# The adaLN product of a hybrid decoder step, spread over four column strips of TensorE

## The chip, the cores and the metric

The kernel runs on one core of a Trainium2 chip. A core has TensorE (matrix products, results in the PSUM memory of eight banks), VectorE, ScalarE and GpSimd (elementwise work; POOL in the profile), and SyncE, whose queue issues the weight loads. The metric is device time in microseconds. TensorE's clock has two levels, 1.2 and 2.4 GHz; the profile shows the granted one as a share of the higher.

## The reference

One inference step of a two-layer trunk for 256 prompt tokens and 8 sequences of 8 sample tokens, all in float32, with D = 1024. Layer 0 is an HGRN2 gated linear recurrence and a dense SwiGLU, layer 1 an S5 state-space mixer and a top-2-of-8 mixture of experts. What matters here is how every sub-layer is modulated:

```python
def _modulation(c, w, b):                       # c: one row per sequence, 1 + 8 = 9 rows
    m = jax.nn.silu(c) @ w + b                  # w: 1024 x 6144, one per layer
    return jnp.split(m[:, None, :], 6, axis=-1) # shift, scale, gate, twice
...
h = _rmsnorm(x, norm_w[layer, 0]) * (1.0 + sc1) + sh1
x = x + g1 * mixer(h)
h = _rmsnorm(x, norm_w[layer, 1]) * (1.0 + sc2) + sh2
x = x + g2 * feed_forward(h)
```

The product silu(c) @ w has 9 rows, a contraction over 1024 and 6144 columns, for each of the two layers.

## The kernel before

Activations are kept transposed: features on the 128 partitions, the 320 tokens along the row. Weights stream from memory through a ring of four slabs, each 128 partitions x 2048 floats (1 MB): eight contraction tiles of 256 output columns. SyncE issues slab n when the first product of slab n - 3 is done (`slab_credit`), so three slabs can be ahead of the one in use.

The adaLN product is cut into 24 pairs of slabs. For each pair q:

- `mod_rows` (line 493) runs twice, once for each half of 256 columns. For each of the eight contraction tiles k it multiplies `siluc[:, k, :]` (128 x 9, the weights of the array) with the slab's tile (128 x 256, streamed) and adds up all eight in PSUM partitions 0 to 8 of one bank. Each float32 matmul is two instructions in the trace, so a slab is 16 and a pair 32.
- ScalarE copies the rows of the bank to `modrow` (line 969, `mod_copy`), which lies in the tile `work`.
- `mod_turn` (line 457, by the helper `tr`) turns four blocks of 9 x 128 into 128 x 9 by a product with the identity, in another bank.
- VectorE adds the bias and writes `mod` (line 1148, `mod_bias`).

The pairs stand in three places of TensorE's order, which is written out by hand:

- Pairs 0 to 3 come at the start, one behind the other. Behind them come the turns of the S5 parameters, the first norm and the HGRN2 input product.
- Pairs 4 to 15 are put between the units of the HGRN2 attention. A unit is one level of a block decomposition of one tile of tokens: VectorE multiplies keys and queries by their decays, TensorE makes the scores (line 607 or 612), VectorE masks them. Units 0 to 3 belong to the sample tokens, 4 to 11 and 12 to 19 to the two prompt tiles. Pairs 4 to 6 follow the scores of units 0 to 2, pairs 7 to 13 those of units 4 to 10, pairs 14 and 15 those of units 12 and 13; a pair's turn stands in the next unit with room. In units 4 to 11 TensorE also makes one head's sample state (line 627, into banks 6 and 7), behind pair and turn, and VectorE adds it before it goes on to the next unit's keys. POOL makes the arguments of the decays up to four units ahead and the mask for line 627; ScalarE takes the exponentials (line 1012).
- Pairs 16 to 23 are put into the S5 loop, one half to each of its 16 steps. There `states_out` (line 750) writes 32 output rows at a time to partitions 32 j to 32 j + 31: four matmuls a step, two for each of two such strips.

Of the kernel before, what the change touches and what calls it, by code (L numbers as in the profile page):

```python
# [20 lines left out]
ACT = mybir.ActivationFunctionType  # L21
AX = mybir.AxisListType

P = 128
D = 1024
KT = D // P
# [6 lines left out]
NC = 1 + NB  # L33
# [10 lines left out]
RING = 4  # L44
# [11 lines left out]
C_KEEP = 392  # L56
C_PAR = 712
C_IOTA = 714
C_W = 842


class Steps:
# [11 lines left out]
def trunk(nc, I, outs, prep):  # L74
    with ExitStack() as ctx:
        def sb(name, shape, dt=F32):
            return ctx.enter_context(nc.sbuf_tensor(name, shape, dt))
# [3 lines left out]
        def sem(name):  # L81
            if name not in sems:
                sems[name] = ctx.enter_context(nc.semaphore(name))
            return sems[name]

        PS = ctx.enter_context(nc.psum_tensor("PS", [P, 8, 512], F32))


        const = sb("const", [P, C_W])
        xT = sb("xT", [P, KT, T])  # L90
        hT = sb("hT", [P, KT, T])
        mod = sb("mod", [P, 96, NC])
        siluc = sb("siluc", [P, KT, NC])
        vecs = sb("vecs", [P, 49])
        adab = sb("adab", [P, 96])
        scale_a = sb("scale_a", [P, KT, NC])
# [4 lines left out]
        work = sb("work", [P, 1024])  # L101
        acts = work[:, 0:2 * T].rearrange("p (s t) -> p s t", s=2)
        gated = work[:, 2 * T:3 * T]
        modrow = work[0:NC, :].rearrange("p (s n) -> p s n", s=2)
        sT = sb("sT", [P, 19, GP])
        ring = sb("ring", [P, RING, SLAB])
        zero16 = sb("zero16", [P, 512], BF16)
# [346 lines left out]
        def _(pe):  # L454
            def tr(out, in_, k):

                return pe.matmul(out, in_, ident[0:k, 0:k], start=True, stop=True)  # L457
# [11 lines left out]
            for k in range(KT):  # L469
                last = tr(PS[:, 5, 16 * k:16 * k + NC], crow[:, k * P:(k + 1) * P], NC)  # L470
            last.then_inc(sem("siluc_psum"), 1)
            pe.wait_ge(sem("ld_x"), 32)
            for i in range(TT):
                for half in range(2):
                    if i == 2:
                        pe.wait_ge(sem("x_turned"), half + 1)
                    for k in range(4):
                        kk = half * 4 + k
                        last = tr(PS[:, 2 * (i % 2) + half, k * P:k * P + TOK[i]],
                                  xin[0:TOK[i], i, kk * P:(kk + 1) * P], TOK[i])  # L480
# [4 lines left out]
            def mod_rows(q, half, bank):  # L485

                n = q * 2 + half
                n += s_mod0 if q in pairs0 else s_mod1 - 8 if q in pairs1 else s_mod2 - 32
                if half == 0 and q:
                    pe.wait_ge(sem("mod_rows_read"), q)  # L490
                arrived(n)
                for k in range(KT):
                    last = pe.matmul(PS[0:NC, bank, half * 256:half * 256 + 256], siluc[:, k, :],  # L493
                                     ring[:, n % RING, k * 256:k * 256 + 256], start=(k == 0), stop=(k == KT - 1))
                    if k == 0:
                        last.then_inc(slab_credit, 1)
                if half:
                    last.then_inc(sem("mod_rows_psum"), 1)

            def mod_turn(q, bank):  # L500
                pe.wait_ge(sem("mod_rows_read"), q + 1)
                if q:
                    pe.wait_ge(sem("mod_ready"), q)
                for c in range(4):
                    last = tr(PS[:, bank, c * NC:(c + 1) * NC], modrow[:, q % 2, c * P:(c + 1) * P], NC)
                last.then_inc(sem("mod_turn_psum"), 1)

            for q in pairs0:
# [8 lines left out]
            for m in range(19):  # L517
                last = tr(PS[:, 4 + m // 10, (m % 10) * GP:(m % 10) * GP + GP], ssr[:, 16 + m, :], GP)
# [16 lines left out]
            for a in range(2):  # L535
                for m in range(2):
                    last = tr(PS[:, 6, (a * 2 + m) * P:(a * 2 + m + 1) * P], x0n[a][:, m, :], P)
            last.then_inc(sem("x0_psum"), 1)

            with pe.Fori(0, 3) as s:  # L540
                for h in range(H):
# [3 lines left out]
                    for k in range(KT):  # L545
                        last = pe.matmul(PS[:, h % 4, 0:T],  # L546
                                         ring[:, h // 2, k * 256 + (h % 2) * P:k * 256 + (h % 2) * P + P],
                                         hT[:, k, :], start=(k == 0), stop=(k == KT - 1))
# [6 lines left out]
            for src in (bexp[0], bexp[1], cexp[0], cexp[1]):  # L555
                for half in range(2):
                    if g >= 4:
                        pe.wait_ge(sem("mats_turned"), g - 3)
                    for k in range(4):
                        last = tr(PS[:, 4 + g % 4, k * P:(k + 1) * P], src[:, half * 4 + k, :], P)  # L560
# [4 lines left out]
            for j in range(4):  # L565
                arrived(s_hin + 12 + j)
                for i in range(TT):
                    pe.wait_ge(sem("hin_credit"), g + 1)
                    for k in range(KT):
                        last = pe.matmul(PS[0:TOK[i], g % 4, 0:256], hT[:, k, i * P:i * P + TOK[i]],  # L570
                                         ring[:, j, k * 256:k * 256 + 256], start=(k == 0), stop=(k == KT - 1))
# [7 lines left out]
            for i in range(TT):  # L579
                for half in range(2):  # L580
                    if g >= 2:
                        pe.wait_ge(sem("kt_ready"), g - 1)
                    for k in range(4):
                        h = half * 4 + k
                        last = tr(PS[0:TOK[i], 6 + g % 2, k * P:(k + 1) * P], hT[:, h, i * P:i * P + TOK[i]], P)
# [3 lines left out]
            for u, (i, L) in enumerate(units):  # L589
                n = TOK[i]  # L590
# [11 lines left out]
                for h in range(H):  # L602
                    kq = ekq[b % 4][:, h, 0:n] if L else None
                    if u in masked:
                        keys, queries = (kq, kq) if L else (x[:, h, i * P:i * P + n] for x in (hk, hq))
                        at = h * n
                        last = pe.matmul(PS[0:n, 2 + at // 512, at % 512:at % 512 + n], keys, queries, start=True,
                                         stop=True, skip_group_check=True)
                        continue
                    for s0 in range(0, P, 2 * L):  # L610
                        c = (h % 4) * P + s0 + L
                        last = pe.matmul(PS[s0:s0 + L, h // 4, c:c + L], kq[:, s0:s0 + L], kq[:, s0 + L:s0 + 2 * L],
                                         start=False, stop=(L == 16 and h % 4 == 3), skip_group_check=True)
# [7 lines left out]
                if u in sample_at:  # L621
# [4 lines left out]
                    for half in range(2):  # L626
                        last = pe.matmul(PS[:, 6 + half, :], hkt[0:64, 2, h * P:(h + 1) * P],  # L627
                                         vmask[0:64, half * 4:half * 4 + 4, :], start=True, stop=True)
# [12 lines left out]
                for part in range(H * n // 512):  # L641
# [3 lines left out]
                    for h in range(part * 512 // n, (part + 1) * 512 // n):  # L645
                        at = (h * n) % 512
                        o = PS[:, 4, at:at + n]
                        last = pe.matmul(o, hv[0:n, i, h * P:(h + 1) * P], scores[0:n, h, 0:n], start=True,
                                         stop=(i == 0), skip_group_check=True)
                        if i == 1:  # L650
                            last = pe.matmul(o, st1[:, h, :], hf[:, h, P:2 * P], start=False, stop=True,
                                             skip_group_check=True)
                        if i == 2:
                            for b in range(NB):
                                last = pe.matmul(o[:, b * NS:(b + 1) * NS], st0[:, b, h, :],
                                                 hf[:, h, NP + b * NS:NP + (b + 1) * NS],
                                                 start=False, stop=(b == NB - 1), skip_group_check=True)
# [11 lines left out]
            for c in range(5):  # L669
                last = pe.matmul(PS[:, c, :], const[:, C_ONE:C_ONE + P], hbflat[:, c * 512:(c + 1) * 512],  # L670
                                 start=True, stop=True)
# [122 lines left out]
            for i in range(TT):  # L794
                n = TOK[i]
# [144 lines left out]
        def _(act):  # L940
# [24 lines left out]
            def mod_copy(q, bank):  # L965
                act.wait_ge(sem("mod_rows_psum"), q + 1)
                if q > 1:
                    act.wait_ge(sem("mod_turn_psum"), q - 1)
                A(modrow[:, q % 2, :], PS[0:NC, bank, :], ACT.Copy).then_inc(sem("mod_rows_read"), 1)  # L969

            for q in pairs0:
                mod_copy(q, q % 2)
# [170 lines left out]
        def _(dve):  # L1143
# [42 lines left out]

            V.memset(epst[:], EPS).then_inc(sem("eps_ready"), 1)
            V.memset(zero16[:], 0.0).then_inc(sem("zeros"), 1)

            dve.wait_ge(sem("ld_ssm"), 48)  # L1190
            dve.wait_ge(sem("dt_ready"), 1)
# [10 lines left out]
            def reduced(out, quarter):  # L1202
# [33 lines left out]
            step(V.tensor_copy(vecs[:], PS[:, 4, 0:49]))  # L1236
            step(V.tensor_copy(adab[:], PS[:, 4, 64:160]))
            dve.wait_ge(sem("siluc_psum"), 1)
            V.tensor_copy(siluc[:], PS[:, 5, 0:128].rearrange("p (k c) -> p k c", k=KT)[:, :, 0:NC])\
                .then_inc(sem("siluc_ready"), 1)  # L1240
            g = 0
            for i in range(TT):
# [435 lines left out]
def constants(np):  # L1678

    c = np.zeros((P, C_W), np.float32)  # L1680
    s = np.arange(P)[:, None]
    t = np.arange(P)[None, :]
    c[:, C_ID:C_ID + P] = s == t
    c[:, C_BEFORE:C_BEFORE + P] = s < t
    c[:, C_ONE:C_ONE + P] = 1
    c[:, C_SAMPLE:C_SAMPLE + NB] = s // NS == t[:, 0:NB]
    keep = np.ones(T, np.float32)
    keep[[0, P]] = 0
    keep[NP::NS] = 0
    c[:, C_KEEP:C_KEEP + T] = keep  # L1690
    c[:, C_PAR:C_PAR + 2] = (s // 16) % 2 == t[:, 0:2]
    c[:, C_IOTA:C_IOTA + P] = t
    return c


# [33 lines left out]
```

## Time and profile before

| | us |
|---|---|
| median of 3 runs | 2364.74 (2363.24 to 2364.99) |
| span of the profiled execution (first to last instruction) | 2361.8 |
| TensorE matmul busy | 1991.8 (84%) |
| VectorE busy | 1209.0 (51%) |
| ScalarE busy | 775.6 (33%) |
| GpSimd busy | 608.9 (26%) |

The time of the profiled execution that is shown is its span; the median of the runs is 2.9 us longer, for what lies around the span. Matmuls are pipelined and their ends modelled, so the durations of single matmuls add up to more than the busy time. Busy shares are means over stages with different limits; what a change in one stage is worth is read from that stage.

### The profile page before, as it was taken

The page shows a single profiled execution, that of the slowest core. Times are in us where ns is not written, and L with a number is a line of the kernel's source. Part 1 is how long each engine was busy: PE and PEld are TensorE (multiplying, and loading weights), DVE is VectorE, ACT ScalarE, POOL GpSimd, SP SyncE. Part 2 cuts the span into 40 slices and gives each one's busy share as a digit, 9 for nine tenths or more (in the row PEclk, how much of TensorE's full clock was granted, in tenths as well). Part 3 has the DMA queues.
Part 4 walks back from the last instruction along what each step waited for, and adds up shares of the span by engine and source line. Part 5 has one row for each costly group of instructions (what it writes and reads, how often), then busy time and mean ns, then how long its engine had stood idle before and what let it go on. Part 6 is the DMA issues. An engine that isn't in the chain of part 4 may idle for free.

```text
span 2361.8 us, 27880 instructions
## 1 busy us (share of the span) xinstructions
PE 1991.8 (84%) x10680; PEld 1510.2 (64%) x10682; DVE 1209.0 (51%) x1486; ACT 775.6 (33%) x813; POOL 608.9 (26%) x308
## 2 busy tenths in 40 slices
PE   5899597665779999566658789999999999999995
PEld 3577463444557767222225579898989898979894
DVE  3300402345220000699991247676767676767675
ACT  1111201011011100111111147575757575757571
POOL 0000201220198000254540003242323232424240
PEclk7799777777789999766668879999999999999998
DMA  5544333320533334121212549898988888888984
GB/s 157 134 116 142 107 107 107 107 76 32 175 104 113 121 105 123 61 72 54 71 54 81 165 133 321 267 320 272 314 285 302 296 298 298 300 297 299 298 301 139
DMA packets 365801, 420.52 MB, mean 178 GB/s; under 512 B 17948, under 2 KB 339757, under 8 KB 365494
## 3 DMA queue, kind: packets, MB, share of 16 engines
q1 hardware_dynamic: 363542, 413.02, 53.5%
q10 hardware_dynamic: 2064, 4.19, 0.6%
q0 software_dynamic: 144, 2.62, 0.3%
q8 instruction: 33, 0.54, 0.1%
q14 instruction: 18, 0.15, 0.0%
HBM read 410.86 MB, written 8.95 MB: 178 GB/s over the span
## 4 chain that ended last, share of the span: by engine, by line
PE 73%; DVE 21%; ACT 3%; issue 2%; DMA 0%; SPq 0%; DVEq 0%; ACTq 0%
PE PS L845 29%; DVE arena L1148 11%; PE PS L697 8%; PE PS L493 5%; PE PS L546 4%; PE PS L457 4%; PE PS L722 4%; PE PS L831 3%; PE PS L784 3%; DVE exact L1148 2%; PE PS L570 2%; DVE arena L1429 2%; DVE hT L1148 2%; PE PS L682 2%; PE PS L527 1%
## 5 line engine op out<-in xcount | busy, mean ns | idle before, releaser
L845 PE MATMUL PS<-exact 128*112 128x256 f32 (+1 forms) x5280 | 774.4, 306 | 19.9 <-DVE exact L1148 19.9
L845 PEld LDWEIGHTS PS<-exact 128*112 128x112 f32 x5280 | 686.9, 175 | 87.8 <-DVE exact L1148 27.7
L1148 DVE TENSOR_TENSOR exact<-arena,exact 128x2048 fp32r<-128x2048 f32 (+1 forms) x162 | 310.9, 1923 | 140.8 <-ACT exact L1087 140.1
L1604 POOL TENSOR_TENSOR arena<-arena 128x512 f32<-128x512 f32 (+4 forms) x154 | 226.4, 1491 | 434.3 <-ACT arena L1056 333.9
L1087 ACT ACTIVATE exact<-arena 128x2048 fp32r<-128x2048 f32 x162 | 309.9, 1913 | 41.5 <-PE PS L845 41.4
L1148 DVE TENSOR_TENSOR arena<-arena 128x128 f32<-128x128 f32 (+7 forms) x399 | 262.1, 709 | 65.4 <-ACT arena L1012 52.2
L1604 POOL TENSOR_TENSOR exact<-arena,exact 128x1024 fp32r<-128x1024 f32 x56 | 192.6, 3446 | 268.3 <-ACT exact L1087 268.3
L1148 DVE TENSOR_TENSOR exact<-ring,exact 128x2048 fp32r<-128x2048 f32 (+1 forms) x104 | 224.9, 2169 | 56.5 <-ACT exact L1087 56.5
L1604 POOL TENSOR_TENSOR exact<-ring,exact 128x1024 fp32r<-128x1024 f32 x32 | 103.9, 3248 | 508.8 <-ACT exact L1087 508.8
L493 PE MATMUL PS<-ring,siluc 128*9 128x256 f32 x768 | 210.7, 441 | 12.5 <-ACT work L969 12.0
L697 PE MATMUL PS<-hT,ring 128*128 128x320 f32 x704 | 191.8, 436 | 14.8 <-DVE hT L1172 14.8
L1087 ACT ACTIVATE exact<-ring 128x2048 fp32r<-128x2048 f32 x104 | 198.0, 1912 | 17.8 <-PE PS L845 17.8
L697 PEld LDWEIGHTS PS<-hT,ring 128*128 128x128 f32 x704 | 134.9, 192 | 71.7 <-DVE hT L1172 15.3
L493 PEld LDWEIGHTS PS<-ring,siluc 128*9 128x9 f32 x768 | 76.2, 102 | 146.4 <-issue 62.8
L1148 DVE TENSOR_TENSOR arena<-arena,PS 112x256 f32<-112x256 f32 (+2 forms) x162 | 79.2, 493 | 97.5 <-PE PS L627 83.5
L457 PE MATMUL PS<-const,arena 112*128 112x112 f32 (+6 forms) x596 | 96.5, 299 | 35.7 <-DVE xT L1245 19.7
L750 PE MATMUL PS<-arena 128*32 128x320 f32 x128 | 36.6, 722 | 98.2 <-DVEq L1434 98.2
L457 PEld LDWEIGHTS PS<-const,arena 112*128 112x128 f32 (+6 forms) x596 | 88.2, 215 | 41.7 <-DVE xT L1245 19.9
L546 PE MATMUL PS<-hT,ring 128*128 128x320 f32 x384 | 105.2, 437 | 0.0
L1148 DVE TENSOR_TENSOR arena<-work,PS 128x320 f32 x22 | 10.7, 488 | 181.8 <-PE PS L697 181.8
L722 PE MATMUL PS<-arena,ring 128*128 128x320 f32 x352 | 95.0, 433 | 1.1 <-DVEq L1403 1.1
L546 PEld LDWEIGHTS PS<-hT,ring 128*128 128x128 f32 x384 | 74.0, 193 | 30.9 <-issue 1.2
(195 smaller groups left out, 1735.1 us busy)
## 6 DMA issues: line engine op xcount, KB each, us to landing
arena<-in_moe_w_in SPq DMA_DIRECT2D x109, 1024.0 KB, 7.5
ring<-in_moe_w_in SPq DMA_DIRECT2D x75, 1024.0 KB, 9.2
arena<-in_moe_w_out SPq DMA_DIRECT2D x56, 1024.0 KB, 5.1
ring<-in_ada_w SPq DMA_DIRECT2D x48, 1024.0 KB, 5.2
ring<-in_moe_w_out SPq DMA_DIRECT2D x33, 1024.0 KB, 7.5
ring<-in_ffn_w_in SPq DMA_DIRECT2D x22, 1024.0 KB, 6.2
ring<-in_hgrn_w_in SPq DMA_DIRECT2D x16, 1024.0 KB, 5.7
ring<-in_ffn_w_out SPq DMA_DIRECT2D x16, 704.0 KB, 5.5
```

The lines of the kernel that those rows point to most:

```text
L457: return pe.matmul(out, in_, ident[0:k, 0:k], start=True, stop=True)
L493: last = pe.matmul(PS[0:NC, bank, half * 256:half * 256 + 256], siluc[:, k, :], ring[:, n % RING, k * 256:k * 256 + 256], start=(k == 0), ...
L546: last = pe.matmul(PS[:, h % 4, 0:T], ring[:, h // 2, k * 256 + (h % 2) * P:k * 256 + (h % 2) * P + P], hT[:, k, :], start=(k == 0), stop= ...
L570: last = pe.matmul(PS[0:TOK[i], g % 4, 0:256], hT[:, k, i * P:i * P + TOK[i]], ring[:, j, k * 256:k * 256 + 256], start=(k == 0), stop=(k ...
L697: last = pe.matmul(PS[:, 2 * (t % 2) + m, 0:T], ring[:, (n + m) % RING, k * 256 + sub * P:k * 256 + sub * P + P], hT[:, k, :], start=(k == ...
L722: last = pe.matmul(PS[:, c, 0:T], ring[:, (n + k // 11) % RING, (k % 11) * P:(k % 11 + 1) * P], mid[:, k, :], start=(k == 0), stop=(k == F ...
L784: last = pe.matmul(PS[:, 2 * sub + m, 0:T], ring[:, (n + m) % RING, k * 256 + sub * P:k * 256 + sub * P + P], hT[:, k, :], start=(k == 0), ...
L831: last = pe.matmul(PS[:, 6 + half, k * P:k * P + CAP], htok[0:TOK[i], i, kk * P:(kk + 1) * P], pick[0:TOK[i], i, :], start=(i == 0), stop= ...
L845: last = pe.matmul(out, a[x], w[y], start=first and m == 0, stop=end and m == 2)
L1087: A(wparts[0][:, j % HRING, :], eslab(j), ACT.Copy).then_inc(sem("rounded"), 1)
L1148: return V.tensor_tensor(out, a, b, op)
L1604: return G.tensor_tensor(out, a, b, op)
```

## The change

The eight contraction tiles of a slab go to four strips of 32 array columns in turn: tile k writes PSUM partitions 32 (k mod 4) to 32 (k mod 4) + 31, and each strip adds up two tiles. For that `siluc` is widened from 9 to 32 columns, the rest zero, cleared once by VectorE. ScalarE copies all 128 partitions of the bank. The turn no longer multiplies with the identity but with a selector: a 128 x 9 block of the constants with a one where partition mod 32 equals the column, so that it turns the rows and adds up the four strips in the same product.

```diff
+C_SEL = 842
-C_W = 842
+C_W = 851
...
-        siluc = sb("siluc", [P, KT, NC])
+        siluc = sb("siluc", [P, KT, 32])
...
-        modrow = work[0:NC, :].rearrange("p (s n) -> p s n", s=2)
+        modrow = work[:].rearrange("p (s n) -> p s n", s=2)
...
                 for k in range(KT):
-                    last = pe.matmul(PS[0:NC, bank, half * 256:half * 256 + 256], siluc[:, k, :],
-                                     ring[:, n % RING, k * 256:k * 256 + 256], start=(k == 0), stop=(k == KT - 1))
+                    strip = 32 * (k % 4)
+                    last = pe.matmul(PS[strip:strip + 32, bank, half * 256:half * 256 + 256], siluc[:, k, :],
+                                     ring[:, n % RING, k * 256:k * 256 + 256], start=(k < 4), stop=(k >= 4))
...
                 for c in range(4):
-                    last = tr(PS[:, bank, c * NC:(c + 1) * NC], modrow[:, q % 2, c * P:(c + 1) * P], NC)
+                    last = pe.matmul(PS[:, bank, c * NC:(c + 1) * NC], modrow[:, q % 2, c * P:(c + 1) * P],
+                                     const[:, C_SEL:C_SEL + NC], start=True, stop=True)
...
-                A(modrow[:, q % 2, :], PS[0:NC, bank, :], ACT.Copy).then_inc(sem("mod_rows_read"), 1)
+                A(modrow[:, q % 2, :], PS[:, bank, :], ACT.Copy).then_inc(sem("mod_rows_read"), 1)
...
             V.memset(zero16[:], 0.0).then_inc(sem("zeros"), 1)
+            step(V.memset(siluc[:], 0.0))
...
-            V.tensor_copy(siluc[:], PS[:, 5, 0:128].rearrange("p (k c) -> p k c", k=KT)[:, :, 0:NC])\
+            V.tensor_copy(siluc[:, :, 0:NC], PS[:, 5, 0:128].rearrange("p (k c) -> p k c", k=KT)[:, :, 0:NC])\
...
+    c[:, C_SEL:C_SEL + NC] = s % 32 == t[:, 0:NC]
```

## Rows read from the trace of the kernel before

**Rows 1.** The page: shares of the chain that ended last, by line.
```profile
PE PS L845 29%; DVE arena L1148 11%; PE PS L697 8%; PE PS L493 5%; PE PS L546 4%; PE PS L457 4%; PE PS L722 4%; PE PS L831 3%; PE PS L784 3%; DVE exact L1148 2%; PE PS L570 2%; DVE arena L1429 2%; DVE hT L1148 2%; PE PS L682 2%; PE PS L527 1%
```
**Rows 2.** The chain in order of time: start, length, engine, tile, line, instructions.
```profile
39.58 9.35 PE PS L493 x32
...
65.64 7.00 PE PS L493 x32
75.32 8.31 PE PS L457 x38
...
313.63 8.69 PE PS L493 x32
```
**Rows 3.** Groups by form, 294 to 540 us: count, busy, mean ns, idle before.
```profile
L493 PE MATMUL PS<-ring,siluc 128*9 128x256 f32 x384 | 93.9, 407 | 0.0
...
L1148 DVE TENSOR_TENSOR arena<-arena,PS 128x1024 f32<-128x1024 f32 x9 | 11.0, 1221 | 83.5 <-PE PS L627 83.5
```
**Rows 4.** The chain through one unit, 381 to 400 us.
```profile
382.56 8.43 PE PS L493 x32
391.00 0.98 PE PS L457 x8
391.98 1.92 PE PS L627 x4
...
394.00 4.97 DVE arena L1148 x3
```
**Rows 5.** Windows: length, busy of five engines, granted clock, DMA share, GB/s.
```profile
1000.00:1258.00 258.00, 155.97 (x535) 61.73 (x533) 238.99 (x428) 38.25 (x129) 123.37 (x84) 0.66 0.18 57
...
1130.00:1135.00 5.00, 2.20 (x8) 0.57 (x8) 4.50 (x14) 0.54 (x4) 1.14 (x1) 0.50 0.00 0
```
**Rows 6.** Timeline of TensorE and its weight loads in one S5 step.
```profile
1132.80 2.35 PE L750 MATMUL PS<-arena 128*32 128x320 f32 x8 [5.60 <-DVEq L1434]
...
1133.34 0.19 PEld L750 LDWEIGHTS PS<-arena 128*32 128x32 f32 x2 [0.34 <-issue]
```
**Rows 7.** Timeline: the scores of unit 6, blocks of 16.
```profile
399.02 0.73 PE L612 MATMUL PS<-arena 128*16 128x16 f32 x64 [5.12 <-DVE arena L1148]
```
**Rows 8.** Timeline: VectorE's first wait, a turn-like product, a ScalarE copy.
```profile
11.11 0.28 DVE L1195 TENSOR_TENSOR arena<-arena 32x128 f32<-32x128 f32 x1 [9.93 <-ACT arena L960]
...
331.31 3.58 PE L655 MATMUL PS<-arena 128*128 128x8 f32 x16
...
359.69 0.60 ACT L1029 ACTIVATE hT<-PS 128x512 f32<-128x512 f32 x1 [36.74 <-PE PS L655]
```
**Rows 9.** The page, DMA issues: KB each, median us to landing.
```profile
ring<-in_ada_w SPq DMA_DIRECT2D x48, 1024.0 KB, 5.2
```
**Rows 10.** Window with a full DMA queue; columns as in rows 5.
```profile
10.00:20.00 10.00, 5.72 (x35) 5.50 (x34) 8.55 (x18) 0.20 (x1) 0.00 (x0) 1.00 0.94 296
```
**Rows 11.** Timeline of SyncE's queue: slab issues, first to last merged.
```profile
40.63 17.95 SPq L321 DMA_DIRECT2D ring<-in_ada_w  x5
...
296.18 23.68 SPq L321 DMA_DIRECT2D ring<-in_ada_w  x6
```
**Rows 12.** Groups by form, 364.4 to 409 us and 419.8 to 486 us.
```profile
L493 PE MATMUL PS<-ring,siluc 128*9 128x256 f32 x96 | 26.2, 441 | 0.0
...
L493 PE MATMUL PS<-ring,siluc 128*9 128x256 f32 x128 | 28.7, 383 | 0.0
```
**Rows 13.** Windows of pairs 7, 9 and 10; columns as in rows 5.
```profile
364.50:373.50 9.00, 9.00 (x34) 3.34 (x33) 0.00 (x0) 0.00 (x0) 0.00 (x0) 0.78 0.55 169
...
399.70:408.10 8.40, 8.40 (x39) 3.07 (x32) 0.50 (x1) 0.00 (x0) 0.00 (x0) 0.83 0.58 184
419.90:427.00 7.10, 7.10 (x34) 2.92 (x34) 0.00 (x0) 0.02 (x1) 0.00 (x0) 1.00 0.69 218
```
**Rows 14.** Timeline: the exponential for unit 7, the scores of unit 7.
```profile
398.44 1.06 ACT L1012 ACTIVATE arena<-arena 128x1024 f32<-128x1024 f32 x1 [6.82 <-POOL arena L1604]
...
416.29 3.65 PE L607 MATMUL PS<-arena 128*128 128x128 f32 x16 [5.25 <-DVE arena L1148]
```

## The prediction

> **What bounds the kernel now.** I read the chain that ended last first. The matmul of line 493, the adaLN product, holds 5% of it [rows 1], so the question is in which of its three places it lies there: before the first norm (pairs 0 to 3), between the units of the attention stage (pairs 4 to 15), or in the S5 loop (pairs 16 to 23). A pair is two weight slabs of 1 MB, 16 matmul instructions each.
>
> Pairs 0 to 3 lie on the chain one behind the other, the first from 39.6 us, the last to 72.6, and the next step after turn and bias starts at 75.3 (first and last of four in [rows 2]). Pairs 4 to 15 take 93.9 us between 294 and 540, and VectorE's state update waits 83.5 us there for the state matmul (line 627), which TensorE issues behind the pair [rows 3]. One unit shows the ring: pair 8.43, turn 0.98, state matmul 1.92, VectorE 4.97, then the next unit's scores [rows 4]. A microsecond off the pair is one off the ring. In the S5 loop VectorE is busy for 239 of 258 us [rows 5]: the pairs there lie beside it, and a shorter pair gives nothing.
>
> **The change, part by part.** *The product.* A pair today is 32 instructions in 7.00 us at the high clock [rows 2]: 0.22 us each, and 0.43 at the low one (1.2 GHz, half of 2.4). They all write one strip of the array's output columns and stand in line. After the change neighbours go to four different strips. Does the chip overlap strips? The S5 output (line 750) writes two strips, 128x320, eight instructions a time. In line they would take 8 x 0.22 x 320/256 = 2.2 us at the high clock, 4.4 at the low. The window shows clock 0.50, and the eight took 2.35 [rows 5, 6]: two at a time, although the code gives all four of one strip first, and the weights of the next two are loaded at 1133.34, when the first two were not yet done. For four strips there are only the 16-column scores: 64 instructions in 0.73 us [rows 7], 11 ns each, where in line at the low clock 16 columns need 27 (430 x 16/256). That is 2.3 at a time at least, and such short ones may be held by issue. Bounds, with 0.2 us for the last to drain: two at a time (3.6 us a pair at the high clock, 7.0 at the low) and four (1.9 and 3.6). I take four, as nothing in the rows limits the streams at two.
>
> The Trainium skill speaks against it ("TensorE: Matmul & The Clock Gate", Part 3, on what overlaps): weight loads overlap running matmuls only when the row group differs, and column strips share all their rows. By that rule the load stands bare. Line 750 shares its rows too, and its loads did not stand bare [rows 6]. The same part measures 2.38 times for three column tiles; as an estimate by that page four would give 3.2, the pair 2.2 us instead of 1.9, and the sum would be 12 x 0.3 = 4 us smaller.
>
> *The rest.* The row copy on ScalarE reads 128 partitions instead of 9; another 128x512 copy takes 0.60 us [rows 8], as this one does. The turn contracts over 128 rows instead of 9: sixteen instructions with 128x128 weights and 8 columns take 3.58 us at the low clock [rows 8], 1.8 for eight, about twice today's 0.98 at the high one [rows 4], so the turn costs what the clock makes it cost and no more. The clearing of siluc (128x256) falls where VectorE waits 9.93 us for its first input [rows 8]; bare, it would be about a third of a microsecond. The constants grow by 9 of 842 columns in a load that is over long before line 493 starts. All at nothing.
>
> *When the pair gets shorter, slabs and clock come next.* A slab lands 5.2 us after its issue [rows 9], and a full queue moves 296 GB/s [rows 10], 3.5 us a slab: 7 us a pair, today's pace of the product. Three slabs wait in the ring when a stretch begins.
>
> **A, pairs 0 to 3.** Slab 3 is issued when slab 0's first product is done, at 40.6 as today [rows 11], and lands at 45.9; with 3.5 each, slab 7 lands at 59.9. Its products (1.9, at the low clock, since TensorE now waits between slabs) end at 61.8. Today's tail, 72.6 to 75.3, is 2.7 us; with 0.8 for slower turns the next step starts at 65.3. Gain 10, bounds 7 (slabs at 4 us) and 13.
>
> **B, pairs 4 to 6.** Slab 3 is issued at 296.2 [rows 11] and lands at 301.4, slab 5 at 308.4; its products end at 309.4 instead of 322.3 [rows 2]. Less a slower turn: gain 12, bounds 9 and 14.
>
> **C, pairs 7 to 13.** Today 26.2 us for the first three and 28.7 for the other four [rows 12]. The granted clock tells why they differ: 0.78 in the first window, 0.83 in the third (the second lies between), 1.00 in the fourth [rows 13]. A window of 9.0 us at 0.78 holds 4.0 us of the low level, one of 8.4 at 0.83 holds 2.9; with the scores ahead (2.0 and 0.7) the clock rose 3.6 to 5.9 us after the unit's first matmul. In the later four the scores alone take 3.65 [rows 14], and the pair finds the high clock. Now the short pair is over before the clock rises in the first three: 26.2 - 3 x 3.6 = 15.4, and I give back half of what a low clock costs the turn (0.8) and the state matmul (1.9), 4 in all. In the later four the rise comes between the pair's start (1.9) and 2.2 us into it (3.0): 28.7 - 4 x 2.5 = 18.7. Gain 30. Bounds: high clock behind every pair, 36.5; low throughout, 54.9 - 7 x 3.6 - 7 x 2.7 = 11.
>
> What is late next in the ring: POOL's arguments and ScalarE's exponential run a unit ahead. The exponential at 398.4 [rows 14] feeds VectorE's products only behind the next state matmul, a unit (17.5 us) after 394.0; with units 5 us shorter some 7 us are left.
>
> **D, pairs 14 and 15.** The last slab is issued about 1.1 us after pair 14 begins at 518.1, lands at 524.4, and its products end at 526 instead of 535.6. Gain 9.5, bounds 6 and 10.5.
>
> Sum: 10 + 12 + 30 + 9.5 = 61.5 us. Span 2361.8 - 61.5 = 2300.3; the median of the runs is 2.9 above the profiled span: **2303 us**.
>
> **Rivals.**
> - *Two strips at a time.* A 8, B 10, C (26.2 - 15.7) + (28.7 - 4 x 4.0) = 23, D 6.5: 47.5 us, 2317. For: the only strips that the trace shows at length are two. Against: [rows 7].
> - *The clock stays low through the attention stage.* A 9, B 9, C 11, D 6, less four later scores at 1.6 more each: 28.5 us, 2336. For: TensorE will be idle for a larger share of each unit, and in today's gaps the clock fell to the low level. Against: scores, pair and state matmul are still some 8 us of matmuls at the low clock, and today's rise came after 3.6 to 5.9.
> - *Strips do not overlap here:* the queue keeps its order and the time is 2365.
> - *Slower: the 32-column weight loads come bare.* Two loads of line 750 take 0.19 us [rows 6]. Loads in line with products in line: 32 x (0.22 + 0.18) = 12.8 us a pair, 5.8 more, on 16 pairs: 2458. It decides from (7.0 - 1.9)/32 = 0.16 us bare per instruction if the streams still overlap; below that the change gains. Against: [rows 6]. The skill's rule above would lead here.
>
> **How the numbers follow.** Four strips with the clock as argued 0.64, two strips 0.10, low clock 0.13, no overlap 0.06, bare loads 0.04, something else slower 0.03. The range reaches from all upper bounds (74 us, 2291) to just short of the low clock's 2336: 2290 to 2332. A measurement of this kernel tells 0.2% (5 us) from no change; all cases with overlap are faster by more: faster 0.87, same 0.06, slower 0.07.
>
> **What would show it.** Matmuls of line 493 starting some 50 ns apart and a pair in 1.9 to 3.6 us. SyncE's slab issues in pairs 0 to 6 some 3.5 us apart, line 493 waiting for slabs there (A, B). Units 4 to 10 each 4 to 5 us shorter, the state matmul still ahead of VectorE's update (C). The S5 loop unchanged at 258 us. I am wrong if line 493 keeps 0.2 us between starts, if state matmul or scores grow by what the pair loses (clock), or if the exponential takes the state matmul's place as VectorE's last wait.

## The result, and the profile after

The change makes the kernel faster: 2294.9 us (median of 4 runs, 2294.33 to 2296.87) against 2364.8, a ratio of 0.9712 [0.9699, 0.9726]. The span fell by 69.0 us, from 2361.8 to 2292.8. The forecast was 2303 (2290 to 2332), so the side, the mechanism and the range held, and 8 us more came than the sum had.

Where the 69 us come from is read by laying the two chains beside each other at places that both have: the start of the same step, in us from the span's start.

| step | before | after | gained up to here | by this stretch |
|---|---|---|---|---|
| turns of the S5 parameters (behind pair 3) | 75.3 | 66.1 | 9.3 | 9.3 |
| HGRN2 input product | 102.4 | 92.8 | 9.7 | 0.4 |
| scores of unit 0 | 294.4 | 283.8 | 10.6 | 0.9 |
| scores of unit 4 (behind pairs 4 to 6) | 362.6 | 340.4 | 22.2 | 11.6 |
| state matmul of unit 11 (behind pairs 7 to 13) | 494.6 | 439.8 | 54.8 | 32.7 |
| outputs of the second prompt tile (behind pairs 14, 15) | 560.9 | 495.1 | 65.8 | 10.9 |
| output product | 601.2 | 535.4 | 65.8 | 0.0 |
| second norm | 642.4 | 575.0 | 67.4 | 1.6 |
| first step of the S5 loop | 998.1 | 928.6 | 69.5 | 2.1 |
| end of the S5 loop | 1257.9 | 1188.5 | 69.4 | -0.1 |

First the product itself. Four lines of the timeline of TensorE and its weight loads answer to [rows 2]: pair 0, then slabs 2, 3 and 7.

```profile
39.47 0.20 PEld L495 LDWEIGHTS PS<-ring,siluc 128*32 128x32 f32 x8 [0.70 <-DVE xT L1249]
39.47 3.64 PE L495 MATMUL PS<-ring,siluc 128*32 128x256 f32 x32 [0.52 <-DVE xT L1249]
39.89 0.20 PEld L495 LDWEIGHTS PS<-ring,siluc 128*32 128x32 f32 x4 [0.23 <-issue]
43.82 1.07 PE L495 MATMUL PS<-ring,siluc 128*32 128x256 f32 x16 [0.72 <-ACT work L972]
47.17 1.94 PE L495 MATMUL PS<-ring,siluc 128*32 128x256 f32 x16 [2.28 <-DMA ring<-in_ada_w]
...
59.80 1.94 PE L495 MATMUL PS<-ring,siluc 128*32 128x256 f32 x16 [1.10 <-DMA ring<-in_ada_w]
61.67 1.88 PE L507 MATMUL PS<-const,work 128*128 128x9 f32 x8
```

At the low clock one instruction takes 0.43 us. Eight weight loads come in the first 0.20 us, and then four more each 0.43 us: four instructions run beside each other, one to a strip, and the next four loads lie under them. A pair takes 3.64 us, a slab 1.94. The product then waits for its slabs, as forecast: the products of slab 3 start at 47.2, where the forecast had it land at 45.9, but slab 7 is done at 61.7 (61.8 in the prediction).

Next the chain in order of time through the attention stage; it answers to [rows 2] and [rows 4].

```profile
285.59 5.42 DMA ring<-in_ada_w
...
291.06 1.07 PE PS L495 x16
...
342.41 2.59 PE PS L495 x32
...
354.05 3.41 PE PS L495 x30
...
366.27 3.51 PE PS L495 x32
369.78 1.81 PE PS L507 x8
371.59 3.72 PE PS L630 x4
375.40 5.10 DVE arena L1151 x3
380.54 3.78 PE PS L610 x16
384.32 2.12 PE PS L495 x32
...
399.44 3.08 PE PS L495 x32
...
415.52 1.88 PE PS L495 x32
...
428.57 2.18 PE PS L495 x32
...
463.17 5.33 DMA ring<-in_ada_w
...
468.55 1.11 PE PS L495 x16
...
535.42 36.21 PE PS L685 x128
...
575.00 6.28 PE PS L530 x16
...
588.50 5.48 DVE hT L1175 x8
```

The ring of a unit is the old one with a shorter pair: pair, turn, state matmul (now line 630), VectorE, next scores. Pairs 7 to 13 took 54.9 us before [rows 12]; now their chain pieces add up to 18.8 (2.59, 3.46 with its first two instructions, which are a piece of their own, 3.51, 2.12, 3.08, 1.88, 2.18). The shortest, 1.88, is a pair wholly at the high clock: 7.00 / 1.88 = 3.7 times faster than in line. Where the clock is low behind the pair, the turn (1.81) and the state matmul (3.72) take nearly twice as long, as in unit 6 here; in unit 7 they take 0.99 and 1.93, as in [rows 4].

The groups by form of 338 to 435 us say what VectorE waits for there: still the state matmul, 50.8 us.

```profile
L1151 DVE TENSOR_TENSOR arena<-arena,PS 128x1024 f32<-128x1024 f32 x7 | 8.6, 1222 | 50.8 <-PE PS L630 50.8
```

Last, windows of the S5 loop and of the first two 3 us of the output product (columns as in [rows 5]).

```profile
535.42:538.42 3.00, 3.00 (x6) 2.02 (x7) 0.00 (x0) 0.00 (x0) 0.00 (x0) 0.50 0.16 31
538.42:541.42 3.00, 3.00 (x13) 2.13 (x12) 0.00 (x0) 0.00 (x0) 0.00 (x0) 1.00 0.96 318
...
930.50:1188.50 258.00, 113.07 (x534) 49.97 (x533) 239.16 (x428) 38.47 (x129) 120.59 (x84) 0.51 0.18 57
```

In the loop TensorE has 43 us less to do (113 against 156), its mean clock fell from 0.66 to 0.51, VectorE is as busy as ever, and the loop takes 259.9 us where it took 259.8 (last two lines of the table).

The 3.7 us behind the attention stage, which no term of the sum had, are in these pieces of the chain of the kernel before, in windows of its output product, and in one window of the second norm's matmuls in each kernel, before and after:

```profile
601.17 37.80 PE PS L682 x128
...
642.35 7.55 PE PS L527 x16
...
657.51 7.11 DVE hT L1172 x8
```
```profile
601.17:604.17 3.00, 3.00 (x6) 2.02 (x7) 0.00 (x0) 0.00 (x0) 0.00 (x0) 0.50 0.14 37
604.17:607.17 3.00, 3.00 (x7) 1.86 (x6) 0.00 (x0) 0.00 (x0) 0.00 (x0) 0.50 0.93 312
...
642.35:646.00 3.65, 3.65 (x7) 2.47 (x8) 0.00 (x0) 0.00 (x0) 3.65 (x3) 0.50 0.82 264
```
```profile
575.00:578.00 3.00, 3.00 (x8) 1.98 (x9) 0.00 (x0) 0.00 (x0) 3.00 (x1) 0.66 0.73 218
```

The output product lost 1.6 us (37.80 to 36.21): the clock rose after 3 us instead of 6. The norm's matmuls lost 1.3 (7.55 to 6.28), and there too the clock rose sooner: the mean granted clock of their first 3 to 4 us was 0.66 instead of 0.50, that of the rest 0.79 instead of 0.70. VectorE's scaling behind them lost 1.6 (7.11 to 5.48). The change touches none of the three. With smaller pieces beside them they come to 4.9 us, of which 1.1 is lost again up to the S5 loop.

For the scaling, the timelines of GpSimd show what ran beside it, before and after:

```profile
661.15 4.44 POOL L1604 TENSOR_TENSOR arena<-arena,sT 128x512 f32<-128x512 f32 x4
```
```profile
589.50 2.73 POOL L1608 TENSOR_TENSOR arena<-arena,sT 128x256 f32<-128x256 f32 x4
```

GpSimd starts work of its own with the second norm in both kernels (at 642.24 and 574.91), in which its instructions grow from 32 to 512 columns. VectorE's eight scalings come behind the norm's matmuls. Before, they started 15.2 us after the norm did, and the last three ran beside instructions of 512 columns, at 1.21 us each. Now they start 13.5 us after it and are done as those begin: 0.88 us at most. In the first norm, where GpSimd is idle, all eight take 2.6 us. So the scaling follows the norm's matmuls, and these follow the clock. It is read from the traces; no run moved GpSimd's work.

### The profile page after: what moved, and what is told of

It is laid out like the page before. It is cut to its first block, busy times and chain, and to the rows that moved or that the text cites. A ratio compares the mean times of both kernels' runs of the same rounds, so it can differ in the third digit from the quotient of the medians.

```text
span 2292.8 us, 27883 instructions
## 1 busy us (share of the span) xinstructions
PE 1871.5 (82%) x10682; PEld 1473.3 (64%) x10682; DVE 1207.8 (53%) x1487; ACT 775.8 (34%) x813; POOL 605.7 (26%) x308
## 4 chain that ended last, share of the span: by engine, by line
PE 71%; DVE 22%; ACT 3%; issue 2%; DMA 1%; SPq 0%; DVEq 0%; ACTq 0%
PE PS L848 30%; DVE arena L1151 12%; PE PS L700 8%; PE PS L549 5%; PE PS L725 4%; PE PS L458 4%; PE PS L834 3%; PE PS L787 3%; DVE exact L1151 2%; PE PS L573 2%; DVE arena L1433 2%; DVE hT L1151 2%; PE PS L685 2%; PE PS L530 1%; PE PS L927 1%
## 5 line engine op out<-in xcount | busy, mean ns | idle before, releaser
L1608 POOL TENSOR_TENSOR arena<-arena 128x512 f32<-128x512 f32 (+4 forms) x154 | 221.4, 1458 | 423.9 <-ACT arena L1059 335.1
L458 PE MATMUL PS<-const,arena 112*128 112x112 f32 (+6 forms) x596 | 97.8, 302 | 34.8 <-DVE xT L1249 18.3
L753 PEld LDWEIGHTS PS<-arena 128*32 128x32 f32 x128 | 9.2, 158 | 170.5 <-DVEq L1438 159.5
L1151 DVE TENSOR_TENSOR arena<-arena,PS 112x256 f32<-112x256 f32 (+2 forms) x162 | 79.1, 492 | 64.9 <-PE PS L630 50.8
L495 PE MATMUL PS<-ring,siluc 128*32 128x256 f32 x768 | 75.7, 544 | 20.6 <-ACT work L972 12.4
```

The source lines that it names most:

```text
L495: last = pe.matmul(PS[strip:strip + 32, bank, half * 256:half * 256 + 256], siluc[:, k, :], ring[:, n % RING, k * 256:k * 256 + 256], star ...
L753: last = pe.matmul(PS[q:q + 32, 4 + k % 2, 0:T], cct[a][:, k, q:q + 32], vb[w % 2][a][:, j, :], start=(a == 0), stop=(a == 1), skip_group_ ...
L1151: return V.tensor_tensor(out, a, b, op)
L1608: return G.tensor_tensor(out, a, b, op)
```

## The experiments

The theory: matmuls that write different strips run beside each other, four at a time; the time they save is worth itself where the pair lies on the chain, until slabs or the clock come next. Rivals: two at a time; a gain from something else in the change (the wider rows, the selector); strips that only help because the code deals them out in turn. Unless said otherwise the edits are to the changed kernel, in three rounds against the kernel before. Its median was 2363.7 us beside the first four kernels, 2360.8 beside the fifth, sixth, seventh and ninth, and 2362 to 2364 beside the others, so ratios compare better than times.

### Two strips

```diff
-                    strip = 32 * (k % 4)
+                    strip = 32 * (k % 2)
...
-    ..., start=(k < 4), stop=(k >= 4))
+    ..., start=(k < 2), stop=(k >= 6))
```
Copy and turn then work on 64 partitions.

> Tiles alternate between two strips instead of four; copy and turn read 64 partitions. If the gain is the overlap of strips, a pair streams in 3.4 us at the high clock and 6.8 at the low instead of 1.7 and 3.4, and the units of the attention stage grow by 1.5 to 2.5 us each, the rest little because slabs bound it: about 14 us more than the changed kernel's 2295, 2305 to 2318. Rival: something holds four strips to the pace of two (reading the slab, issue): 2295, no difference.

2307.5 us, 0.976 [0.9744, 0.9776]. Pairs 7 to 13 by form:

```profile
L495 PE MATMUL PS<-ring,siluc 128*32 128x256 f32 x224 | 31.2, 440 | 0.0
```

31.2 us against 54.9 in line and 19.6 with four (18.8 on the chain). From the scores of unit 4 to the state matmul of unit 11 it takes 106.9 us; that took 132.0 before and takes 99.3 with four strips. So the number of strips sets the pace. The second pair of strips is worth less than the first (12 against 56 us): a second halving takes half of what the first took, and slabs and clock hold back part of it.

### The strips in blocks

```diff
-                    strip = 32 * (k % 4)
+                    strip = 32 * (k // 2)
...
-    ..., start=(k < 4), stop=(k >= 4))
+    ..., start=(k % 2 == 0), stop=(k % 2 == 1))
```

> Four strips, but two neighbouring tiles (four instructions) go to the same strip before the next strip's turn. Theory: each strip has its own line and the queue lets a later strip's matmul start past waiting ones, as line 750 seemed to show: 2295 as with strips in rotation, matmuls of four strips within 50 ns of each other. Rival: matmuls start strictly in program order; then only the last of one strip overlaps the first of the next, 26 steps instead of 32 in a pair, 5.6 us instead of 7.0: 2340 to 2350.

2295.4 us, 0.9712 [0.9695, 0.9728]: the same as with the strips in turn. Timeline of its first pair:

```profile
39.52 0.23 PEld L495 LDWEIGHTS PS<-ring,siluc 128*32 128x32 f32 x8 [0.70 <-DVE xT L1249]
39.53 3.33 PE L495 MATMUL PS<-ring,siluc 128*32 128x256 f32 x32 [0.52 <-DVE xT L1249]
39.95 0.22 PEld L495 LDWEIGHTS PS<-ring,siluc 128*32 128x32 f32 x4 [0.20 <-issue]
```

Here the first four instructions of the code all go to strip 0. If matmuls started in the order of the code, the second strip could not begin before the fourth of them, 3 x 0.43 = 1.3 us in, and the loads of the other strips' products would come later still. They come eight at once and then mostly by fours, four matmuls start between 39.53 and 39.57 and the next four from 39.95 to 40.00, and the pair takes 3.33 us. A strip does not wait for instructions of another that stand ahead of it in the code.

### One strip

```diff
-                    strip = 32 * (k % 4)
+                    strip = 0
...
-    ..., start=(k < 4), stop=(k >= 4))
+    ..., start=(k == 0), stop=(k == KT - 1))
```
Copy and turn work on 32 partitions; the 32-column weights, the selector and the clearing of `siluc` stay.

> Everything of the change but the spreading: 32-column weights, selector in the turn, cleared siluc, all tiles in one strip; copy and turn read 32 partitions. Theory: the whole gain is the overlap, and the rest costs nothing: 2365 plus or minus 3. Rival: part of the gain comes from elsewhere (turn, copy): 2350 or less. Rival: the wider weights cost time bare: over 2375.

2364.2 us, 1.000 [0.9991, 1.001], over ten runs. Pairs 7 to 13 by form:

```profile
L495 PE MATMUL PS<-ring,siluc 128*32 128x256 f32 x224 | 54.6, 406 | 0.0
```

54.6 us, as before. Without the spread, the rest of the change costs and brings nothing; the whole gain is the strips. And 32-column loads are not bare. What this run leaves out, copy and turn on all 128 partitions, is seen in the changed kernel: the copy takes 0.60 us, the turn 0.99 at the high clock, against 0.60 and 0.98 before.

### The spread in one place alone

First in pairs 0 to 3 only; the other pairs keep nine columns and one strip:

```diff
+                    spread = q in pairs0
+                    strip = 32 * (k % 4) if spread else 0
+                    rows = 32 if spread else NC
```

> Only pairs 0 to 3 are spread over strips; the others keep one strip of 9 columns. The difference of the two traces at the first turn of the S5 parameters is 9.3 us (75.3 against 66.1): theory, slab supply bounds it and nothing is lost later: 2354 to 2357. Rival: the earlier start is given back behind it (the clock, the loads of the S5 matrices and of the next weights): over 2360.

2352.9 us, 0.995 [0.9933, 0.9967]: 10.8 less than the kernel before in the median, 8.7 less in the span, and 1 us under the range expected. Then in the pairs of the S5 loop only (`q in pairs2`):

> Only pairs 16 to 23, in the S5 loop, are spread. Theory: VectorE bounds that loop, nothing is gained: 2365 plus or minus 3, loop 258 us, although TensorE's busy time and granted clock fall there. Rival: the lower clock makes states_out or the turn late for VectorE: slower by 5 us or more. Rival: TensorE does matter: faster by 5 us or more.

2362.9 us over ten runs, 1.0012 [1.0001, 1.0022]. A window over the loop in that kernel:

```profile
998.70:1256.60 257.90, 112.99 (x535) 50.01 (x533) 239.04 (x428) 38.49 (x129) 120.58 (x84) 0.51 0.18 57
```

The same product, 8 of the 24 pairs, shortened by the same factor, gives nothing where VectorE is busy 239 of 258 us. What is left of the gain, about 60 us, lies in the attention stage and behind it; this is by subtraction and by the table, as those pairs were not spread alone.

### Slabs sooner

Is it the slabs that the product now waits for? All four slabs of the ring may be ahead, with a credit when a slab is given up rather than when its successor's product begins:

```diff
-            pe.sem_inc(slab_credit, RING - 1)
+            pe.sem_inc(slab_credit, RING)
...
-                    if k == 0:
+                    if k == 0 and q in pairs2 or k == KT - 1 and not half and q not in pairs2:
...
+                if q not in pairs2 and q not in (pairs0[-1], pairs1[-1]):
+                    act.sem_inc(slab_credit, 1)
```
The second half's credit comes from ScalarE behind its wait for the pair's product, and TensorE gives the one for the last pair of a stretch.

> The changed kernel with four slabs ahead instead of three: a slab of pairs 0 to 15 frees its place with its own last product (the second of a pair by ScalarE, once it sees the pair done) instead of the next slab's first. Theory: slab supply is what line 493 now waits for (18.6 us in ten waits in the changed kernel's trace): pairs 0 to 3 end some 3 us earlier, the wait of 5.4 us in pair 5 goes and about 4 of it is kept, the 5.3 us in pair 15 go: 10 to 13 us less, 2282 to 2285. Rival: another chain (VectorE's keys, ScalarE's exponentials) comes at the same time: under 4 us less.

2288.3 us, 0.969 [0.9674, 0.9706]: a gain of 6.6 us (5.2 by the ratios) where 10 to 13 were expected. What the waits of line 495 show in the changed kernel and in this one:

```profile
  DMA ring<-in_ada_w: 18.6, 10
```
```profile
  DMA ring<-in_ada_w: 8.2, 6
```

Ten waits of 18.6 us became six of 8.2, and up to the outputs of the second tile the kernel is 9 us ahead: the input product starts at 90.0 instead of 92.8, unit 0 to the first outputs takes 17.2 instead of 20.6, and unit 12 to the second outputs 30.9 instead of 33.8. The last of these had been expected to give the whole slab wait, 5.3. The chain around pair 14 shows what came next:

```profile
456.64 1.91 PE PS L495 x32
...
458.66 0.60 ACT work L975
459.26 0.95 ACT arena L1018
...
460.23 3.03 DVE arena L1154 x2
```

ScalarE's copy of the rows stands ahead of the exponential for the next keys: the exponential became the last wait, which the prediction had named as what would come next, in a later part of the attention stage than it had looked at. (One pair later, copy and exponential stood on the chain one behind the other in both kernels already, from 535.64 and from 469.68.) And the 3.7 us behind the attention stage were gone again in this kernel: output product 37.74, the norm's matmuls 7.51, scaling 7.11, as in the kernel before.

### Zeros to hold the clock

Behind each state matmul of the units that carry a pair, 18 products of zeros in bfloat16, into a bank that is free there; they add work and change no result:

```diff
+                    if u in mod_at:
+                        pe.wait_ge(sem("mod_rows_read"), mod_at[u] + 1)
+                        for _ in range(18):
+                            pe.matmul(PS[:, 5, :], zero16[:, 0:P], zero16[:], start=True, stop=True)
```

> The changed kernel with 18 extra bf16 matmuls of zeros (128x512) behind the state matmul of units 4 to 10, into the bank that the pair just left, to keep TensorE streaming while VectorE works; they change no result. Theory: the clock is what units 4 to 10 still pay. With the high clock throughout, pairs 18.8 to 13.2 us, scores of units 5 to 10 some 7 us less, turn and state matmul of unit 6 2.6 less: 12 to 16 us less, 2279 to 2283. Rival: the zeros do not raise the clock, or they stand in the way of the next scores: 2295 or more.

2285.4 us, 0.968 [0.9664, 0.9697]. Groups by form in units 4 to 10: pairs and scores, first of the changed kernel, then with zeros.

```profile
L495 PE MATMUL PS<-ring,siluc 128*32 128x256 f32 x224 | 19.6, 507 | 0.0
...
L610 PE MATMUL PS<-arena 128*128 128x128 f32 x80 | 18.6, 426 | 25.1 <-DVE hT L1151 13.5 <-DVE arena L1151 11.6
```
```profile
L495 PE MATMUL PS<-ring,siluc 128*32 128x256 f32 x224 | 15.5, 422 | 0.0
...
L610 PE MATMUL PS<-arena 128*128 128x128 f32 x80 | 12.4, 319 | 6.5 <-DVE arena L1155 3.6 <-DVE hT L1155 2.9
```

4.1 and 6.2 us less, and 1.8 less in the state matmuls: from the scores of unit 4 to the state matmul of unit 11 it took 87.2 us, 12.1 less, at the low end of what was expected. 2.4 of it was given back between unit 11 and the outputs, so the time missed the expected 2279 to 2283. The low clock was thus a cost that still lay in this stage after the change. Was it in the kernel before too? The same zeros put into that:

> The kernel before with the same 18 extra matmuls of zeros. Theory: the clock's price was there before as well, 4.8 us in the first three pairs and some 7 in the scores of units 5 to 10: 10 to 13 us less than before, 2352 to 2355. Rival: the long pair already held the clock high enough, so the price appears only with the change: 2362 or more.

2350.5 us, 0.9955 [0.9938, 0.9971], some 2 us under the range expected. Units 4 to 10 gained 8.9 us there (132.0 to 123.1), less than the 12.1 of the changed kernel. So some 3 us of the clock's cost came with the change; that the shorter pair, which leaves TensorE idle for more of each unit, is the reason is argued and has no run of its own.

### Both

> Four slabs ahead and the 18 matmuls of zeros together. In the traces the first took 9 us off up to unit 20 (2.6 before the input product, 3.4 in pairs 4 to 6, 2.9 in pairs 14 and 15) and lost 3.7 behind the attention stage; the second took 12 off units 4 to 10 and lost 2 in the second prompt tile. Theory: supply and clock are separate terms and add up: 2273 to 2280. Rival: they share a wait: 2284 or more.

2276.2 us, 0.9635 [0.9619, 0.9651]: 18 to 19 us below the change (by ratio, by time), as expected. Up to the output product early slabs alone are 8.7 us ahead of the changed kernel, zeros alone 10.6, and both 18.3: the two add up but for 1 us. Early slabs alone lost some of their gain behind the attention stage; here output product, norm and scaling have the short lengths again (36.21, 6.28, 5.49).

### The clock of the output product

90 more zero products in front of the output product, in the changed kernel and in the version with both:

> The changed kernel with 90 bf16 matmuls of zeros in front of the HGRN2 output product (line 685), in the 22 us in which TensorE waits for VectorE there; they change no result. Theory: what the change gained behind the attention stage without touching it (3.7 us) is how early the clock rose in that product, by chance of its start; with the clock high from the start the product takes 34.2 to 34.6 us instead of 36.2 (37.8 before): 2290 to 2294. Rival: the 3.7 us are something else (slabs, VectorE): product 36 us or more, time unchanged.

> All three together on top of the change. If supply and the clock in the two places are separate, the sum of what each took: 2268 to 2276, with the output product at 34.2 to 34.6 us. If the clock's gain is lost again behind it, as with four slabs ahead: 2278 or more.

2295.2 and 2276.5 us: nothing in either, and both just above what was expected of them (2290 to 2294, 2268 to 2276). In the first, the window and the timeline of the product's start:

```profile
536.80:539.80 3.00, 2.96 (x6) 1.98 (x7) 0.00 (x0) 0.00 (x0) 0.00 (x0) 0.50 0.14 28
```
```profile
536.84 11.59 PE L687 MATMUL PS<-hT,ring 128*128 128x320 f32 x36 [5.03 <-DVE hT L1392]
```

The zeros were over 5.03 us before the product could begin, and the clock was at the low level again when it did. So the version with both was run with 110 instead of 90:

> As the three together, with 110 instead of 90 matmuls of zeros in front of the output product, so that they end some 0.5 us before it starts; 90 ended 5.0 us before, and the clock fell to 0.50 as the product began. Theory: the product then runs at the high clock from the start, 34.2 to 34.6 us instead of 36.2, and the first norm behind it is no longer: 2272 to 2275 against 2276 for the two others together. Rival: the clock falls again in the product or the 3.7 us were something else: 36 us, 2276 or more.

2276.0 us, 0.9635 [0.9621, 0.9648], not the expected 2272 to 2275. Window over the product, and the chain behind it:

```profile
517.20:553.00 35.80, 35.09 (x130) 24.24 (x128) 6.92 (x22) 0.00 (x0) 0.00 (x0) 1.00 0.66 198
```
```profile
518.30 34.73 PE PS L692 x128
...
556.41 7.46 PE PS L530 x16
...
571.53 7.11 DVE hT L1184 x8
```

The product was at the high clock throughout, 0.71 us behind the zeros, and took 34.73 us, 1.5 less, close to what was expected. The norm's matmuls and VectorE's scaling went back to 7.46 and 7.11, and the total did not move. Over all fourteen kernels these two go together: 7.46 to 7.55 with 7.11 or 7.12 in six, among them the kernel before, and 6.28 with 5.17 to 5.50 in eight, among them the changed one. Here the norm's first 3.6 us have the granted clock 0.50, and the scaling runs beside GpSimd's 512-column instructions, as in the kernel before. Why the clock rises sooner in one kernel's norm than in another's stays open.

## Why the prediction was right

**The streams.** Four at a time, the bound that was taken. Shown three ways: the loads by fours, two strips at 2307.5, and one strip at 2364.2. The Trainium skill ("TensorE: Matmul & The Clock Gate", Part 3) lets a load overlap only when the row group differs, and its Part 2 keeps matmuls in program order. The four strips share all their rows, and their loads lay under the products; the blocks of the second experiment ran as fast as the turns. Against both of these sentences the measurement decides here. Part 3 also has 2.38 times for three column tiles, from which the prediction worked out an estimate of 3.2 for four: four gave 3.7 here, and no run has three.

**The rest at nothing.** Right: 1.000 with one strip, and copy and turn of the changed kernel as long as before.

**A, forecast 10.** 9.3. Slabs paced it, and slab 7 was done within 0.1 us of the forecast, in part by luck: the products of slab 3 began 1.3 us later than it was to land, and the four behind it came faster than 3.5 us each. The tail from there to the next step is 4.3 us instead of 2.7 + 0.8: two turns lie in it, those of pairs 2 and 3, and at the low clock each takes 1.88 instead of about 1.0; the prediction had counted one.

**B, forecast 12.** 11.6, with the first slab wait, 5.42, where it was put. Pair 6, which was to wait as well, took 3.44 us without a wait.

**C, forecast 30.** 32.7, the largest miss of the four terms. The pairs were taken at 3 x 3.6 + 4 x 2.5 = 20.8 us; they took 18.8, as the high clock came back sooner in pair 7 (2.59) and in three of the last four. Turns and state matmuls were to give back 4; they gave 2.6 us, in unit 6 alone (1.81 + 3.72 against 0.98 + 1.92). Against that, 0.8 went to scores and one VectorE instruction, which no part of the sum had. The step that was mis-sized is thus the clock, not the streams. That the clock was a cost here is shown by the zeros, which took 12.1 us out of the same units.

**D, forecast 9.5.** 10.9. The last slab was issued 0.7 us into pair 14 instead of 1.1, landed 5.33 later, and its product was over 7.2 us after the pair began, where 7.9 was forecast. Most of the rest lies ahead of the pair: the scores of unit 12 took 1.15 us instead of 1.97.

**The S5 loop, forecast nothing.** Nothing, with the clock of the stage down from 0.66 to 0.51. Its own experiment gave 1.0012.

**What was left out.** 3.7 us behind the attention stage, 0.9 from the input projection to unit 0 and 0.4 before it. The sum is 9.3 + 11.6 + 32.7 + 10.9 = 64.5, and 5.0 with these: 69.5 against the 61.5 of the forecast. The 3.7 come and go: they are there in the changed kernel, in the one with two strips and in the ones with zeros, and were gone in the one with early slabs. For 1.6 of them the trace shows the clock's rise in the output product, 3 us sooner, for 1.3 an earlier rise in the norm, and for 1.6 the scaling that then met shorter GpSimd instructions; 1.1 was lost again. They are no property of the strips that could be forecast, and so a part larger than the shortfall of C is luck of the clock.

**The rivals.** Two strips: forecast 2317, measured at 2307.5 when the code made it so. Its terms were too small in the same way as those of the forecast, by 9 us. A clock low throughout: no; one unit of seven had it behind the pair. No overlap and bare loads: no.

## What to carry to other kernels

A product with few output rows (32 or fewer) leaves three quarters of the array's columns unused; dealing its contraction over four strips and adding them up in a product that follows anyway (here the turn) made it 3.7 times faster at no cost elsewhere. Before it is done, look stage by stage where the product lies on the chain: the same edit gave 9 us in four pairs and nothing in eight. Afterwards the next limits are the supply of slabs and the clock of a TensorE that has become idler, and both could be had back in part (5 to 10 us each) with more slabs ahead and products of zeros.

## What the runs showed of the hardware

- Strips run as separate lines. They need not be dealt out in turn: four instructions (two tiles) to one strip before the next gave 2295.4 us, in turn 2294.9.
- A float32 product of 256 columns is two instructions, each 0.43 us at the low clock and 0.22 at the high one; four strips make 32 of them 1.88 us.
- With 18 bfloat16 products of zeros a unit the granted clock was 1.00 in units 5 to 7, which had 0.64, 0.50 and 0.73 without them; in units 4 and 8 it was 0.85 and 0.87. After a pause of 5.03 us behind 90 such products the next product began at 0.50, after one of 0.71 us at 1.00.
- An output product of 128 instructions took 37.80, 36.21 or 34.73 us, by whether the clock rose 6 us into it, 3 us into it, or was high from the start.
- Eight VectorE instructions of 128x256 took 2.6 us where GpSimd was idle, 5.48 or 7.11 beside GpSimd instructions: 0.78 us each beside those of 256 columns that take 0.62, 1.21 beside those of 512 that take 1.05, the two starting together.
